# GpSimd's feed-forward sums dealt out one to a slot, and four expert units gathered by transfers instead of products

## The chip, the core and the metric

The kernel runs on one core of a Trainium2 chip. A core has five engines with instruction queues of their own: TensorE (PE; its weight loads are shown as PEld), VectorE (DVE), ScalarE (ACT), GpSimd (POOL) and SyncE (SP). Here SP issues nearly all transfers from memory. The metric is the device time of one launch in microseconds. Everything is computed in fp32.

## What is computed

A two-layer transformer block is followed by a second block whose layers end in a mixture of experts. Two parts of it matter here. The first is the squared-ReLU feed-forward at the end of each of the first block's two layers:

```python
h2 = _rmsnorm(h_res, ln2_g[layer])
h_res = h_res + jnp.square(jax.nn.relu(h2 @ w_ff1[layer])) @ w_ff2[layer]
```

The second is the routed part of the two mixtures of experts: 256 tokens, 64 experts, six experts for each token.

```python
def step(acc, xs):
    e, rt, rw = xs
    xb = xf[rt]                                       # the rows of the tokens that chose expert e
    hb = jax.nn.silu(xb @ w_gate[e]) * (xb @ w_up[e])
    yb = (hb @ w_down[e]).astype(F32) * rw[:, None]
    return acc.at[rt].add(yb), None
```

A token is a row of 1024 numbers, and an expert's gate, up and down weights are 1 MiB each.

## The kernel before

**The feed-forward: 32 slots a layer.** Each of the two products is cut into 16 slots, 32 in all, numbered n. A slot multiplies one 1 MiB piece of weights by seven products in place of eight (Strassen's scheme, in a form that reuses partial sums). So it needs combinations of the four quarters of its weights ("mixed") and of the four quarters of the activations ("sums"). In a slot TensorE makes 28 matmuls, in seven groups of four. They begin once VectorE has joined the results of slot n-2, the third group waits for VectorE's `("mixed", L, n)`, and the last group but one waits for GpSimd's.

Per slot, VectorE adds up the seven results (`joined`, L1929 to L1940, four operations, each of which reads PSUM). Then it makes two of the four weight combinations of slot n+2 (`mixed`, L1912 and L1914), the first of which waits for GpSimd's first one. In three slots of four it also does one part of an unrelated job, the modulation weights of the second block (`ada_part`, two operations of 1024 columns, L1712), with a small bias addition after the third (L1717). GpSimd makes the other two weight combinations of each slot (L3170, L3171) as soon as the weights have landed and slot n-2 has been used. In slots 5, 9, 13 and 17 it also combines eight rows of the activations that slots 0 to 15 have produced, in four operations (L3179, L3181, L3182, L3184). Slots 16 to 19 are the first that read those.

SP issues the weights in groups of four slots (L3244), each once slot n-4 is used. Behind each group it waits for VectorE to have finished the last three `ada_part`s and then issues three more MiB of modulation weights (L3249). Its queue is in order.

**The experts: 27 units a layer.** Unit u (0 to 26) handles 128 gathered rows in groups of 32. Each unit has a kind that says how many experts share its 128 rows: `HALVES` (two experts, 64 rows each), `MOST` (two experts, 96 and 32) or `FOUR` (four experts). Units 1 to 25 are five bodies of five, of the kinds HALVES, FOUR, MOST, MOST, HALVES. A unit on TensorE is: the gate and up products of its own rows; the down product of unit u-1; the gather of the rows for unit u+1, in two halves with an `add_up` between them that adds unit u-2's results into the tokens; the row numbers of unit u+2; the other `add_up`; and the transposition of the hidden values. VectorE copies the row numbers out (L2438) and, for a unit that gathers by transfer, also writes them as indices (L2443), which releases GpSimd's indirect transfer (L3209). That transfer goes into one buffer, `M_XT`, and is at most one unit ahead.

A gather is made in one of two ways. By products: eight matmuls of 128 columns in each half, of the tokens in SBUF with a matrix of ones and zeros (L600). By transfer: the 128 rows are fetched from memory and turned with four transpositions in each half (L605). `one_hot(u)` says which. In unit 3 of each body (u = 8, 13, 18, 23) the gather for the next unit, when made by products, is put ahead of the down product:

```python
ahead = one_hot(u + 1) and u > SHARED_UP and (u - 1) % len(BODY) == AHEAD_OF_DOWN
```

Unit 2 also makes tables, unit 3 the shared expert's up product and unit 4 its down product.

The expert weights come through a ring of 13 slots of 1 MiB. SP issues load n once the load n-13 has been used by TensorE (L3298), in order. A body needs 36 loads.

Of the kernel before, what the change touches and what calls it, by code (L numbers as in the profile page):

```python
# [71 lines left out]

def one_hot(u):

    return 1 < u < UNITS - 1 and (u - 1) % len(BODY) in ONE_HOT_PLACES


def fetches(u):
# [209 lines left out]
def build(nc, io, out_ap, known):  # L288
# [2861 lines left out]
    def gpsimd_program():  # L3150
        PE, VE, AC = PES[0], VES[0], ACS[0]
        for L in range(DEPTH):
            if L:
                po.wait_ge(VE.sem, VE.of("ff2 ends", L - 1))
            po.wait_ge(PE.sem, PE.of("x square sums", L))
            POS.up(po.memset(QTM, 0.0))
            POS.up(po.memset(KTM, 0.0), "mla zeroed", L)
            po.wait_ge(PE.sem, PE.of("mla", L, MLA_H - 1, "out"))
            POS.up(po.memset(DQ, 0.0))
            POS.up(po.memset(DK, 0.0), "diff zeroed", L)  # L3160
            for n in range(32):
                po.wait_ge(*dense.landed(FF_AT[L] + n))
                if n == 0:
                    po.wait_ge(VE.sem, VE.of("o normed", L))
                elif n == 1:
                    po.wait_ge(VE.sem, VE.of("attended", L, 4))
                else:
                    po.wait_ge(PE.sem, PE.of("ff used", L, n - 2))
                b11, b12, b21, b22 = quarters(FF_AT[L] + n)
                POS.up(po.tensor_tensor(MIXED[n % 2][0], b12, b11, ALU.subtract), "mixed 1", L, n)  # L3170
                POS.up(po.tensor_tensor(MIXED[n % 2][2], b22, b12, ALU.subtract), "mixed", L, n)  # L3171
                if n in (5, 9, 13, 17):
                    i = (n - 5) // 4
                    t0, t1, width = halves(L)
                    rows = F[:, 8 * i:8 * i + 8, :]
                    a11, a12, a21, a22 = rows[:, 0:4, t0], rows[:, 4:8, t0], rows[:, 0:4, t1], rows[:, 4:8, t1]
                    s1, s2, s4 = [x[:, i, :, 0:width] for x in (S_ONE, S_TWO, S_FOUR)]
                    po.wait_ge(AC.sem, AC.of("ff1 squared", L, 4 * i + 3))
                    POS.up(po.tensor_tensor(s1, a21, a22, ALU.add))  # L3179
                    po.wait_ge(POS.sem, POS.n)  # L3180
                    POS.up(po.tensor_tensor(a21, a11, a21, ALU.subtract))  # L3181
                    POS.up(po.tensor_tensor(s2, s1, a11, ALU.subtract))  # L3182
                    po.wait_ge(POS.sem, POS.n)
                    POS.up(po.tensor_tensor(s4, a12, s2, ALU.subtract), "ff2 sums", L, i)  # L3184
        po.wait_ge(VE.sem, VE.of("even rb", 2))
        po.wait_ge(AC.sem, AC.of("even rb", 3))
        po.dma_start(skew, E_RB).then_inc(skew_stored, 16)
        po.wait_ge(skew_stored, 16)
        for h in range(4):
            for o, n, c0 in ((255, P, 0), (127, 2 * P, P)):  # L3190
                src = bass.AP(tensor=skew.tensor, offset=512 * h + o, ap=[[4 * 512 - 1, P], [1, n]])
                po.dma_start(E_BIAS[:, h, c0:c0 + n], src).then_inc(skew_loaded, 16)

        def moe_layer(L):
            PE, VE, AC = PES[L], VES[L], ACS[L]
            if L == 0:
                po.wait_ge(VE.sem, VE.of("even mix"))
            else:
                po.wait_ge(PE.sem, PE.of("odd o", 1, 1, 1))
            POS.up(po.memset(M_XT, 0.0), "tokens zeroed", L)  # L3200
            for t in range(2):
                po.wait_ge(AC.sem, AC.of("ht", L, t, 1))
                po.dma_start(tokens[L][t * P:(t + 1) * P], M_HT[:, t, :]).then_inc(tokens_stored[L], 16)
            po.wait_ge(POS.sem, POS.of("tokens zeroed", L))
            po.wait_ge(tokens_stored[L], 32)

            def fetch(column):

                po.indirect_dma_start(M_XT, None, tokens[L],  # L3209
                                      bass.IndirectOffsetOnAxis(M_IX[:, column:column + 1], 0), bounds_check=SEQ - 1,  # L3210
                                      oob_is_err=False).then_inc(tokens_landed[L], 16)

            def numbers_made():
                po.wait_ge(numbered[L], 1)
                po.sem_clear(numbered[L])

            po.wait_ge(first_numbered[L], 1)
            fetch(1)
            with po.Fori(0, fetches(UNITS) - 1) as i:
                numbers_made()  # L3220
                fetch(0)
            po.wait_ge(VE.sem, VE.of("turns", L))
            turns = po.value_load(NTI[0:1, L:L + 1], min_val=1, max_val=1 + NOV // 2)
            with po.Fori(0, turns) as i:
                numbers_made()
                fetch(0)

        for L in range(DEPTH):
            moe_layer(L)
# [181 lines left out]
```

## Time and profile before

| | us |
|---|---|
| median of 3 runs | 2589.15 |
| lowest and highest | 2588.43 and 2592.13 |
| the profiled execution, its own time | 2594.4 |
| its span, from first to last instruction | 2593.1 |

The profiled execution is 5.3 us above the median, and 1.3 us of it lie outside the span. The feed-forward slots lie at about 366 to 582 us of the span (first layer) and 916 to 1130 us (second). The units 1 to 26 of the experts lie at about 1321 to 1794 us and at 2094 to 2566 us.

### The profile page before, as it was taken

What the parts mean: (1) busy time and instruction counts of PE and PEld (TensorE: products, weight loads), DVE (VectorE), ACT (ScalarE), POOL (GpSimd) and SP (SyncE); (2) the same over time, 40 slices, a digit from 0 to 9 for tenths busy, and PEclk for the clock granted to TensorE, in tenths of its full rate; (3) what the DMA queues carried; (4) which work ended last, traced back from release to release, by engine and by line L of the source; (5) the groups of instructions that cost most, each with busy time, mean ns of one, the idle gap of its engine ahead of it and who ended that gap; (6) DMA issues with size and microseconds to landing.
All of it is one profiled execution on the core that took longest, in us unless ns stands there. A gap on an engine that the chain in (4) does not pass through costs nothing.

```text
span 2593.1 us, 50004 instructions
## 1 busy us (share of the span) xinstructions
PE 2523.5 (97%) x21294; PEld 1976.6 (76%) x21294; DVE 1102.9 (43%) x2368; ACT 506.7 (20%) x1110; POOL 277.3 (11%) x213
## 2 busy tenths in 40 slices
PE   9999999999999999999999999999999899999998
PEld 6787789997788899988866666665888766666665
DVE  4546448875455378853321111112674321111112
ACT  2323312102333122011210111111342210111102
POOL 0000016630000046410000000000000000000000
PEclk9999999999999999999899999999999999999999
DMA  5223346763233466755389999996331589999995
GB/s 201 95 98 114 114 180 259 293 255 122 95 112 115 145 269 254 310 201 221 145 335 380 390 420 419 419 420 277 116 114 51 227 349 375 400 420 419 419 420 206
DMA packets 96028, 659.58 MB, mean 254 GB/s; under 512 B 12878, under 2 KB 14430, under 8 KB 17728
## 3 DMA queue, kind: packets, MB, share of 16 engines
q1 hardware_dynamic: 90736, 647.28, 62.8%
q0 software_dynamic: 4784, 8.80, 1.0%
q8 instruction: 169, 2.77, 0.4%
q14 instruction: 51, 0.42, 0.0%
q10 hardware_dynamic: 288, 0.31, 0.0%
HBM read 660.92 MB, written 4.19 MB: 256 GB/s over the span
## 4 chain that ended last, share of the span: by engine, by line
PE 89%; DVE 3%; DMA 3%; POOL 2%; ACT 2%; issue 1%; SPq 0%; DVEq 0%; POOLq 0%; ACTq 0%
PE PS L600 85%; PE PS L605 4%; ACT AR L2613 1%; DMA AR<-in_experts 1%; DMA wmoe<-in_experts 1%; DMA wdense<-in_experts 1%; DVE wmoe L1712 1%; DVE wmoe L1912 1%; POOL AR L3181 1%; DVE wmoe L1914 1%; DMA wdense<-in_dense 0%; POOL AR L3179 0%; POOL wmoe L3170 0%; POOL AR L3182 0%; POOL wmoe L3184 0%
## 5 line engine op out<-in xcount | busy, mean ns | idle before, releaser
L600 PE MATMUL PS<-H,wdense 128*128 128x256 f32 (+4 forms) x2432 | 515.3, 368 | 6.4 <-ACT H L2613 2.2
L600 PE MATMUL PS<-AR 128*128 128x128 f32 (+12 forms) x4848 | 498.7, 312 | 14.9 <-ACT AR L2613 10.0
L600 PEld LDWEIGHTS PS<-H,wdense 128*128 128x128 f32 (+1 forms) x2432 | 422.7, 192 | 75.2 <-issue 10.6
L600 PEld LDWEIGHTS PS<-AR 128*32 128x32 f32 (+5 forms) x4848 | 353.2, 148 | 134.7 <-issue 71.5
L2613 ACT ACTIVATE AR<-PS 128x256 f32<-128x256 f32 (+11 forms) x433 | 185.6, 437 | 1343.5 <-PE PS L600 999.4
L600 PE MATMUL PS<-wmoe,AR 128*32 128x256 f32 (+4 forms) x3280 | 343.7, 413 | 5.8 <-DMA wmoe<-in_experts 5.6
L600 PE MATMUL PS<-AR,wdense 128*128 128x256 f32 (+3 forms) x1472 | 283.6, 348 | 2.2 <-DVE AR L2359 2.2
L600 PE MATMUL PS<-AR,CST 128*128 128x256 f32 (+3 forms) x1096 | 271.6, 387 | 12.8 <-ACT AR L2613 12.8
L600 PEld LDWEIGHTS PS<-AR,wdense 128*128 128x128 f32 x1472 | 243.9, 191 | 33.1 <-DVE AR L2359 3.1
L600 PE MATMUL PS<-wdense,AR 128*32 128x256 f32 (+7 forms) x2112 | 257.0, 420 | 1.8 <-DMA wdense<-in_experts 1.3
L600 PEld LDWEIGHTS PS<-wmoe,AR 128*32 128x32 f32 (+2 forms) x3280 | 166.0, 119 | 116.4 <-issue 51.8
L600 PEld LDWEIGHTS PS<-AR,CST 128*128 128x128 f32 (+1 forms) x1096 | 194.3, 189 | 49.6 <-issue 11.1
L600 PEld LDWEIGHTS PS<-wdense,AR 128*32 128x32 f32 (+3 forms) x2112 | 119.1, 118 | 85.6 <-issue 40.9
L2537 DVE TENSOR_TENSOR AR<-AR,PS 128x256 f32<-128x256 f32 x54 | 22.8, 421 | 365.6 <-ACT AR L2613 365.6
L600 PE MATMUL PS<-wdense,H 128*16 128x64 f32 (+3 forms) x1632 | 168.7, 285 | 0.0
L600 PE MATMUL PS<-AR,wmoe 128*128 128x136 f32 (+5 forms) x1472 | 155.6, 271 | 10.3 <-DVE wmoe L1914 10.1
L600 PEld LDWEIGHTS PS<-wdense,H 128*16 128x16 f32 (+1 forms) x1632 | 141.2, 137 | 21.3 <-issue 4.1
L600 PEld LDWEIGHTS PS<-AR,wmoe 128*128 128x128 f32 (+3 forms) x1472 | 140.1, 174 | 20.0 <-DVE wmoe L1914 11.6
L3170 POOL TENSOR_TENSOR wmoe<-wdense 128x512 f32<-128x512 f32 x64 | 89.5, 1398 | 600.9 <-DMA wdense<-in_dense 420.9
L2613 ACT ACTIVATE AR<-AR 128x272 f32<-128x272 f32 (+13 forms) x207 | 124.1, 621 | 106.1 <-DVE AR L1841 40.1
L1712 DVE SCALAR_TENSOR_TENSOR wmoe<-wmoe 128x1024 f32<-128x1024 f32 x96 | 130.8, 1401 | 0.0
L3209 POOL DMA_INDIRECT AR<-tokens,IX x26 | 25.9, 996 | 970.2 <-DVE IX L2443 940.7
(318 smaller groups left out, 2049.1 us busy)
## 6 DMA issues: line engine op xcount, KB each, us to landing
wmoe<-in_experts SPq DMA_DIRECT2D x180, 1024.0 KB, 17.1
wdense<-in_dense SPq DMA_DIRECT2D x172, 1024.0 KB, 4.8
wdense<-in_experts SPq DMA_DIRECT2D x114, 1024.0 KB, 17.7
AR<-in_experts SPq DMA_DIRECT2D x90, 1024.0 KB, 17.1
wmoe<-in_ada SPq DMA_DIRECT2D x48, 1024.0 KB, 8.4
AR<-in_dense SPq DMA_DIRECT2D x4, 1024.0 KB, 7.5
tokens<-AR POOLq DMA_DIRECT2D x4, 512.0 KB, 4.0
wdense<-in_dense SPq DMA_DIRECT2D x2, 768.0 KB, 9.3
```

Source lines behind the costliest of these rows:

```text
L600: return te.matmul(out, lhsT, rhs, start=start, stop=stop, skip_group_check=True)
L605: return te.matmul(out, src, ident[0:n, 0:n], start=True, stop=True, is_transpose=True, skip_group_check=True)
L1712: VE.up(ve.scalar_tensor_tensor(w, w, 1.0, CROW, ALU.mult, ALU.mult, accum_out=MODS[:, at(2 * s + g, 1)]))
L1912: VE.up(ve.tensor_tensor(m2, b22, m1, ALU.subtract))
L1914: VE.up(ve.tensor_tensor(m4, b21, m2, ALU.subtract), "mixed", L, n)
L2537: VE.up(ve.tensor_tensor(M_HM, M_HM, PS[:, B_GU, 0:256], ALU.mult))
L2613: return ac.activation(dst, src, f, bias=bias, scale=scale)
L3170: POS.up(po.tensor_tensor(MIXED[n % 2][0], b12, b11, ALU.subtract), "mixed 1", L, n)
L3181: POS.up(po.tensor_tensor(a21, a11, a21, ALU.subtract))
L3209: po.indirect_dma_start(M_XT, None, tokens[L], bass.IndirectOffsetOnAxis(M_IX[:, column:column + 1], 0), bounds_check=SEQ - 1, oob_is_err= ...
```

## The change

GpSimd's four operations for a block of eight activation rows no longer stand together in slots 5, 9, 13 and 17. One stands behind the two weight combinations of each slot from 5 on. The last block has two in slot 17 and two in slot 18. The other edit is `one_hot`: units 2, 3, 4 and 24 are now gathered by transfer, so that 11 units of a layer instead of 15 are gathered by products. Unit 23 no longer gathers ahead of its down product.

```diff
-    return 1 < u < UNITS - 1 and (u - 1) % len(BODY) in ONE_HOT_PLACES
+    return len(BODY) < u < UNITS - 3 and (u - 1) % len(BODY) in ONE_HOT_PLACES
```

```diff
-                if n in (5, 9, 13, 17):
-                    i = (n - 5) // 4
+                if 5 <= n < 19:
+                    i, r = (n - 5) // 4, (n - 5) % 4
...
-                    po.wait_ge(AC.sem, AC.of("ff1 squared", L, 4 * i + 3))
-                    POS.up(po.tensor_tensor(s1, a21, a22, ALU.add))
-                    po.wait_ge(POS.sem, POS.n)
-                    POS.up(po.tensor_tensor(a21, a11, a21, ALU.subtract))
-                    POS.up(po.tensor_tensor(s2, s1, a11, ALU.subtract))
-                    po.wait_ge(POS.sem, POS.n)
-                    POS.up(po.tensor_tensor(s4, a12, s2, ALU.subtract), "ff2 sums", L, i)
+                    steps = [(s1, a21, a22, ALU.add), (a21, a11, a21, ALU.subtract), (s2, s1, a11, ALU.subtract), (s4, a12, s2, ALU.subtract)]
+                    if r == 0:
+                        po.wait_ge(AC.sem, AC.of("ff1 squared", L, 4 * i + 3))
+                    for j in (range(2 * r, 2 * r + 2) if i == 3 else range(r, r + 1)):
+                        out, x, y, how = steps[j]
+                        if j in (1, 3):
+                            po.wait_ge(POS.sem, POS.n)
+                        POS.up(po.tensor_tensor(out, x, y, how), "ff2 sums", L, i)
```

GpSimd's queue in the first layer, slots 5 and 6 before (L3170 and L3171 are a slot's weight combinations, the others are the four sums):

```order
L3170 TENSOR_TENSOR wmoe<-wdense 128x512
L3171 TENSOR_TENSOR AR<-wdense 128x512
L3179 TENSOR_TENSOR AR<-AR 128x544
L3181 TENSOR_TENSOR AR<-AR 128x4x136
L3182 TENSOR_TENSOR AR<-AR 128x544
L3184 TENSOR_TENSOR wmoe<-AR 128x544
L3170 TENSOR_TENSOR wmoe<-wdense 128x512
L3171 TENSOR_TENSOR wmoe<-wdense 128x512
```

and slots 5 to 8 after, where the sums are all line L3185:

```order
L3170 TENSOR_TENSOR wmoe<-wdense 128x512
L3171 TENSOR_TENSOR AR<-wdense 128x512
L3185 TENSOR_TENSOR AR<-AR 128x544
L3170 TENSOR_TENSOR wmoe<-wdense 128x512
L3171 TENSOR_TENSOR wmoe<-wdense 128x512
L3185 TENSOR_TENSOR AR<-AR 128x4x136
L3170 TENSOR_TENSOR wmoe<-wdense 128x512
L3171 TENSOR_TENSOR AR<-wdense 128x512
L3185 TENSOR_TENSOR AR<-AR 128x544
L3170 TENSOR_TENSOR wmoe<-wdense 128x512
L3171 TENSOR_TENSOR wmoe<-wdense 128x512
L3185 TENSOR_TENSOR wmoe<-AR 128x544
```

The same four sums now have a pair of weight combinations between each two of them.

TensorE's queue at the end of unit 1, where the rows of unit 2 are gathered (AR x AR is the product with ones and zeros, CST is the unit matrix of a transposition or a result in `add_up`):

```order
-L600 MATMUL PS<-AR 128x128 x8
-L600 MATMUL PS<-AR,CST 128x256 x4
-L600 MATMUL PS<-AR 128x128 x8
+L605 MATMUL PS<-CST,AR 128x128 x4
+L600 MATMUL PS<-AR,CST 128x256 x4
+L605 MATMUL PS<-CST,AR 128x128 x4
 L600 MATMUL PS<-AR 32x2 x8
```

Sixteen matmuls became eight transpositions in the same place. It is the same in units 2 and 3.

In unit 23 the sixteen stood between the gate and up products and the down product (the operations of 512 columns):

```order
 L600 MATMUL PS<-wdense,AR 32x256 x33
-L600 MATMUL PS<-AR 128x128 x16
 L600 MATMUL PS<-wdense,AR 32x512
 L600 MATMUL PS<-wmoe,AR 32x512 x3
```

They left that place, and the eight transpositions stand behind the down product, around `add_up`. VectorE gets one operation more, L2443, in units 0, 1, 2 and 22, and GpSimd one indirect transfer more behind each.

## Rows read from the trace of the kernel before

**Rows 1.** Waits of TensorE: for whom; us in total, times, longest.
```profile
PE PS L600 <- DVE wmoe L1914: 10.1, 8, 1.4
PE PS L600 <- DMA wmoe<-in_experts: 5.6, 2, 2.8
```

**Rows 2.** Timeline of TensorE, feed-forward: start, us, instruction, [idle before <- releaser].
```profile
437.74 1.19 PE L600 MATMUL PS<-AR,wmoe 128*128 128x136 f32 x8 [1.18 <-DVE wmoe L1914]
...
468.94 1.09 PE L600 MATMUL PS<-wmoe,wdense 128*128 128x136 f32 x8
...
475.43 1.09 PE L600 MATMUL PS<-wmoe,wdense 128*128 128x136 f32 x8
```

**Rows 3.** Timeline of GpSimd, slots 9 and 10 of the first layer.
```profile
426.35 1.64 POOL L3179 TENSOR_TENSOR AR<-AR 128x544 f32<-128x544 f32 x1 [1.97 <-ACT AR L2613]
428.06 2.21 POOL L3181 TENSOR_TENSOR AR<-AR 128x544 f32<-128x544 f32 x1
...
431.65 1.34 POOL L3184 TENSOR_TENSOR wmoe<-AR 128x544 f32<-128x544 f32 x1
432.96 1.26 POOL L3170 TENSOR_TENSOR wmoe<-wdense 128x512 f32<-128x512 f32 x1
```

**Rows 4.** Timeline of VectorE in the same slots.
```profile
425.57 1.22 DVE L1712 SCALAR_TENSOR_TENSOR wmoe<-wmoe 128x1024 f32<-128x1024 f32 x1
...
426.71 2.35 DVE L1712 SCALAR_TENSOR_TENSOR wmoe<-wmoe 128x1024 f32<-128x1024 f32 x1
...
430.42 0.44 DVE L1934 TENSOR_TENSOR AR<-AR,PS 128x272 f32<-128x272 f32 x1
...
434.26 1.75 DVE L1912 TENSOR_TENSOR wmoe<-wdense,wmoe 128x512 f32<-128x512 f32 x1 [2.12 <-POOL wmoe L3170]
...
439.45 0.68 DVE L1912 TENSOR_TENSOR AR<-wdense,wmoe 128x512 f32<-128x512 f32 x1
```

**Rows 5.** L3244's weight load issued at 430.4, the first behind three modulation loads.
```profile
DMA to landing us min/median/max: 12.2/12.2/12.2
```

**Rows 6.** Timeline of VectorE, experts: copies of row numbers, one per unit (0, 5 to 9).
```profile
1320.70 0.16 DVE L2438 COPY AR<-PS 128x2 f32<-128x2 f32 x1 [1.41 <-PE PS L600]
...
1420.99 0.16 DVE L2438 COPY AR<-PS 128x2 f32<-128x2 f32 x1 [2.30 <-PE PS L600]
...
1439.36 0.16 DVE L2438 COPY AR<-PS 128x2 f32<-128x2 f32 x1 [5.06 <-PE PS L600]
...
1457.86 0.16 DVE L2438 COPY AR<-PS 128x2 f32<-128x2 f32 x1 [5.06 <-PE PS L600]
...
1477.58 0.15 DVE L2438 COPY AR<-PS 128x2 f32<-128x2 f32 x1
...
1493.19 0.15 DVE L2438 COPY AR<-PS 128x2 f32<-128x2 f32 x1
```

**Rows 7.** Timeline of TensorE: the first half of a gather, by products and by transpositions.
```profile
1331.42 2.05 PE L600 MATMUL PS<-AR 128*128 128x128 f32 x16
...
1489.98 0.66 PE L605 MATMUL PS<-CST,AR 128*128 128x128 f32 x4
```

**Rows 8.** Windows, first layer's experts: stretch, busy us by engine, clock, DMA share, GB/s.
```profile
1320.00:1405.00 85.00, 85.00 (x870) 58.65 (x868) 15.96 (x49) 7.80 (x17) 1.01 (x1) 1.00 1.00 413
1405.00:1452.00 47.00, 47.00 (x455) 29.41 (x449) 9.02 (x24) 5.25 (x11) 0.99 (x1) 1.00 0.84 323
1452.00:1712.00 260.00, 254.87 (x2688) 165.81 (x2686) 47.10 (x123) 29.04 (x59) 5.93 (x6) 1.00 1.01 420
```

**Rows 9.** GpSimd's 26 indirect transfers, line L3209.
```profile
DMA to landing us min/median/max: 2.1/8.1/9.3
```

**Rows 10.** Expert load issued at 1733.7 (second down weights of unit 23).
```profile
DMA to landing us min/median/max: 21.1/21.1/21.1
```

**Rows 11.** Timeline of TensorE: a down product, and unit 24's gather behind its down product.
```profile
1391.60 3.62 PE L600 MATMUL PS<-AR 128*32 128x512 f32 x32
...
1759.88 0.66 PE L605 MATMUL PS<-CST,AR 128*128 128x128 f32 x4
```

## The prediction

> **What bounds the kernel now.** I read the waits of TensorE first, then the timelines of the two places that the change touches, then how fast the transfers run there. TensorE is busy nearly all the time, so time can only be won where TensorE waits, or by taking work from it. Of the waits two bear on this change [rows 1]: 10.1 us in eight waits for VectorE's second weight combination (L1914), and 5.6 us in two waits for expert weights. The eight waits are one for each of the four bunches of sums in each of two layers. At 426.35 GpSimd starts its four sums for slot 9, at 432.96 it is at last at the weights of slot 10 [rows 3], VectorE begins its part of them at 434.26 [rows 4], and TensorE stands for 1.18 us until 437.74 [rows 2]. A slot without a wait is 6.5 us (468.94 to 475.43, the same group of matmuls one slot apart [rows 2]), so four slots are 26.0 and a period with one bunch of sums 27.3.
>
> The expert stage has two bounds that lie close together. By TensorE a unit of the second body takes 15.6 to 19.7 us [rows 6]. The transfers run at 413 GB/s from 1320 to 1405, at 323 from 1405 to 1452, and at 420 from there on, which is all they ever give [rows 8]. So at first TensorE sets the pace and later the transfers do.
>
> **Part one, gathers: TensorE's side.** Unit 6 gathers by products and takes 18.37 us (1420.99 to 1439.36), unit 9 by transfer and takes 15.61 (1477.58 to 1493.19) [rows 6]: 2.76 us less. The halves say the same: 2.05 us busy against 0.66 [rows 7], twice 1.4. Three units of the first body (1, 2 and 3, which gather for 2, 3 and 4) make 3 x 2.75 = 8.2 us in a layer. Unit 23 has today's form of unit 8, with the products ahead of the down product: 19.72 us (1457.86 to 1477.58) [rows 6]. It becomes like unit 9, 4.1 us less. Together 12.3 us less work for TensorE in a layer.
>
> **Part one: what the transfers let through.** The 36 loads of a body do not get fewer, so TensorE's 8.2 us count only if the transfers still have time to spare before they saturate. From 1320 to 1405 they leave (420 - 413)/420 x 85 = 1.4 us unused, from 1405 to 1452 (420 - 323)/420 x 47 = 10.9 [rows 8], together 12.3. The change takes 8.2 of that away. It adds three token transfers of 0.5 MB, at 420 GB/s 1.25 us each if they cost their bytes, 3.7 in all. 8.2 + 3.7 = 11.9 is less than 12.3: the gain passes in full, and everything behind it, the saturated stretch too, starts 8.2 us earlier. It is a close sum, though. Had the spare time been 8 us, nearly half of the gain would be gone. A bound from the other end is a token transfer that costs nothing, with 4.1 us to spare and the same 8.2.
>
> For unit 23 the transfers are saturated. The second down weights of unit 23 were issued at 1733.7 and landed 21.1 us later [rows 10], at 1754.8. TensorE asks for them when unit 24's down product starts, at 1759.88 less 3.6 = 1756.3 [rows 11]. So they are 1.5 us early, and of the 4.1 us only 1.5 come through; the rest turns into a wait for a transfer. Ends: 0 and 4.1.
>
> Do the fetched rows come in time? Unit 1 is the tightest, since it has one `add_up` less in front. Its row numbers are copied at 1320.70 [rows 6] and its gather starts at 1331.42 [rows 7], 10.7 us later. A fetch takes 8.1 us from issue to landing, 9.3 at most [rows 9], which leaves 1.4 to 2.6 us for VectorE's index write and GpSimd's start. I cost the wait at 0; at the other end it is 1 us in a layer. The write and the start lie on engines that are nearly idle here (16.0 and 1.0 us busy of 85 [rows 8]), and TensorE has 12 us of other work meanwhile. Should the wait come, the slots of the ring behind it come free later by as much.
>
> On that transfer the Trainium skill gives a formula (DMA: Bandwidth & Descriptors, "Anatomy of one DMA"): about 2.0 us plus the bytes over 436 GB/s, for half a MiB an estimate of 3.2 us. The trace disagrees, with its 8.1 us among expert loads, and only its 2.1 us at the least would fit an idle queue. By the page the rows could never be late; by the trace they just aren't, and the measurement decides.
>
> Gathers in all: -(8.2 + 1.5) = -9.7 us a layer, -19.4 for both.
>
> **Part two, the sums dealt out.** At first sight this wins all 10.1 us: a slot has 6.5 us, GpSimd's two weight combinations take 2.5 of them (1.26 each) and one sum 1.34 more [rows 3]. But GpSimd and VectorE stop each other. VectorE's modulation step takes 1.22 us alone; the one that starts at 426.71 takes 2.35 [rows 4]. It ends at 429.06, and GpSimd's L3179 ended at 427.99 [rows 3]: it did nothing until then and took its 1.07 us after. In turn L3181 takes 2.21 us, where L3184 takes 1.34: it began at 428.06 and got going when VectorE ended. L1912 takes 1.75 us beside GpSimd and 0.68 alone, while the `joined` operations keep their 0.44 beside it (430.42) [rows 4]: they read PSUM. So operations of the two engines that only read SBUF run one after the other, and each meeting costs VectorE up to 1.1 us.
>
> VectorE's work in four slots, alone: four `joined` of 4 operations (up to 0.44, with gaps 1.7) 6.8; four pairs of combinations (0.68 each) 5.6; six modulation steps of 1.22, 7.3; gaps and the bias step 0.9. That is 20.6 us of 26.0. I laid out the queues of both engines slot by slot in either order, with these durations and that rule. In the old order VectorE waits 5.4 us for GpSimd in a period; 20.6 + 5.4 = 26.0 fits into 27.3, and the layout gives the TensorE wait as 1.30 us a bunch, against 1.18 in the row [rows 2]. In the new order every sum stands where VectorE is in its second combination or in a modulation step, and the waits are 6.8, 7.4 and 8.7 us in the first three periods. 20.6 + 7.4 = 28.0 does not fit into 26.0. VectorE falls back by 2 us a period. For two periods nobody sees it, and TensorE wins 1.3 us twice. In the third TensorE must wait for `joined` (results of slot n-2) and the period is 28.8. In the fourth, with its two sums in slots 17 and 18, it is 27.7 against 27.2. In slot 21 TensorE then waits 2.0 us. First layer: -1.3 - 1.3 + 1.5 + 0.5 + 2.0 = +1.4. In the second layer, where a slot is 0.23 us shorter and VectorE's work hardly less, the same layout gives +3.2. Sum +4.6, which I round to +5.
>
> The sums themselves come early enough: the last two stand behind the weights of slot 18, and slot 19 is the first that reads them. GpSimd's wait for ScalarE (1.97 us [rows 3]) stays in slots 5, 9, 13 and 17, with one sum behind it in place of four.
>
> What gets late next is known too. SP issues three modulation loads only after VectorE's last step of the four, and the next weights stand behind them: 12.2 us from issue to landing [rows 5], against the two slots, 13.0 us, until GpSimd can use them. Every us by which VectorE falls back passes nearly whole into those weights. A landing 1.2 us late makes the sum 3 us worse in a layer. Bounds of part two: -10.1 (no meeting matters) and +11 (VectorE falls back and the weights come late in both layers). I take +5, since it is by these very rows; it lies between.
>
> The Trainium skill has this as a rule (SBUF — State Buffer, "Who interferes with whom"): GpSimd and a VectorE operation with two SBUF inputs share a port pair as an exclusive lock, held for the whole instruction, and the other one blocks. The trace agrees, with 2.35 for 1.22 us.
>
> **Sum.** The profiled execution took 2594.4 us, span 2593.1: 2594.4 - 19.4 + 5.0 = 2580.0. It lies 5.3 above the median of the runs, so against that median 2589.15 - 14.4 = **2574.7**.
>
> **Rivals.**
> 1. *The sums leave the path for good*: the meetings happen but VectorE catches up where it has no modulation step. For it: one slot in four has none. Against it: the balance of 28.0 us against 26.0. 2589.15 - 19.4 - 10.1 = 2559.6.
> 2. *Late weights*: VectorE's delay comes back through SP's queue, part two costs +11. For it: 12.2 of 13 us [rows 5]. 2580.7.
> 3. *Part two is nought, or unit 23's 4.1 us come through*: 2570.
> 4. *The other side: the transfers bind from the start of the units.* Then TensorE's 12.3 us only lengthen its waits for loads, and eight fetches of 1.25 us are added to a stream that is full: +10, with part two +15, 2604. It decides at the spare transfer time: 12.3 us now, 11.9 needed; it would need fewer than 4. Against it: 323 GB/s from 1405 to 1452 [rows 8].
>
> **How the numbers follow.** The forecast 0.50, rival 1 0.20, rival 2 0.15, rival 3 0.09, rival 4 0.06. The forecast's own range, with the ends of unit 23 and of the fetches, is 2568 to 2580. To leave no more than 2 in 10 out, the range goes from rival 1 to a little above rival 2: 2559 to 2583. About 0.2% (5.2 us) is what a measurement can tell from no change. Faster by more: 0.88; within: 0.06; slower: 0.06.
>
> **What would show it.** Right: 64 more transpositions (L605) and 128 fewer products of 128 columns (L600); units 1, 2 and 3 are 2.75 us shorter; the rate from 1405 to 1452 rises towards 420 GB/s; a wait for expert weights of 1 to 3 us appears behind unit 23; L1712 has more operations of 2.3 us than now; TensorE's waits on L1914 do not vanish but move to the later slots, some of them on L1940. Wrong: no waits of TensorE on VectorE in the slots (rival 1), GpSimd waiting for `wdense` in slots 8, 12 and 16 (rival 2), or unit 1 waiting for its tokens.

## The result, and the profile after

The changed kernel takes 2573.85 us (median of 4 runs, 2572.99 to 2576.02), where before takes 2588.79 (4 runs, 2588.37 to 2592.13): 14.9 us less, a ratio of 0.9941 with a 95% interval of 0.9929 to 0.9954. The forecast was 2574.7, 14.4 less than the 2589.15 that it started from.

The two profiled executions differ by more, 2593.1 against 2571.8 of span. So the parts are read stage by stage. First the expert units. Timeline of VectorE, the copies of row numbers at the end of units 0 to 3, 22 and 23, first layer of after (start, us, operation):

```profile
1320.09 0.15 DVE L2438 COPY AR<-PS 128x2 f32<-128x2 f32 x1
1333.94 0.15 DVE L2438 COPY AR<-PS 128x2 f32<-128x2 f32 x1
1350.99 0.15 DVE L2438 COPY AR<-PS 128x2 f32<-128x2 f32 x1
1373.84 0.15 DVE L2438 COPY AR<-PS 128x2 f32<-128x2 f32 x1
...
1718.44 0.15 DVE L2438 COPY AR<-PS 128x2 f32<-128x2 f32 x1
1736.83 0.15 DVE L2438 COPY AR<-PS 128x2 f32<-128x2 f32 x1
```

Units 1, 2 and 3 take 13.85, 17.05 and 22.85 us. Before they took 16.59, 19.79 and 25.59: each is 2.74 shorter, in both layers. Unit 23 takes 18.39 where it took 19.64, and 17.75 in the second layer. (Where VectorE writes the numbers as indices first, L2443, the copy comes 0.08 us later. That is taken out here.) Unit 17 takes 0.67 less in the first layer and 0.89 more in the second, units 22 and 24 up to 0.2 more. The 26 units give 9.96 us in the first layer and 8.94 in the second, 18.9 together.

Only part of this repeats. Nine more traces, of the experiments below, have the same gathers. Units 1 to 3 are as short in every one. Units 17 and 22 to 24 come out otherwise each time, and against the 946.0 us of before the 26 units of both layers give from 14.0 to 18.1 us in them. The 18.9 of after are the most of the ten, and 16.9 is their mean.

Three windows of after, which answer to [rows 8] (stretch, busy us by engine, clock, DMA share, GB/s):

```profile
1320.00:1405.00 85.00, 85.00 (x850) 55.76 (x852) 17.38 (x57) 8.23 (x17) 4.96 (x5) 1.00 1.02 420
1405.00:1452.00 47.00, 47.00 (x456) 30.88 (x454) 9.64 (x24) 5.88 (x12) 0.00 (x0) 1.00 1.00 413
1452.00:1712.00 260.00, 254.12 (x2688) 162.03 (x2676) 46.94 (x121) 27.85 (x57) 5.93 (x6) 0.99 1.01 420
```

The spare time is used up: 413 became 420 and 323 became 413. Of 12.3 us some 0.8 are left. The 34 indirect transfers (line L3210 of after, [rows 9]) now take

```profile
DMA to landing us min/median/max: 2.1/8.6/10.3
```

Now the feed-forward. TensorE's waits in the whole of after, those that answer to [rows 1] (us in total, times, longest):

```profile
PE PS L600 <- DMA wmoe<-in_experts: 10.0, 4, 2.8
PE PS L600 <- DVE wmoe L1914: 8.1, 7, 2.6
...
PE PS L600 <- DVE AR L1940: 4.2, 5, 1.1
PE PS L600 <- DVE AR L1914: 2.7, 4, 1.9
```

On VectorE TensorE waits 15.0 us in the slots, where before it waited 12.0 (10.1, and 1.9 once on L1914 writing `AR`). The waits moved to later slots, and five are now on `joined` (L1940). The timeline of TensorE shows all those of the first layer; the one in slot 6 is gone:

```profile
436.83 1.19 PE L600 MATMUL PS<-AR,wmoe 128*128 128x136 f32 x8 [0.89 <-DVE wmoe L1914]
...
455.85 2.12 PE L600 MATMUL PS<-H,wdense 128*128 128x136 f32 x16 [1.14 <-DVE AR L1940]
...
463.59 2.12 PE L600 MATMUL PS<-H,wdense 128*128 128x136 f32 x16 [0.99 <-DVE AR L1940]
...
466.59 1.19 PE L600 MATMUL PS<-AR,wmoe 128*128 128x136 f32 x8 [0.89 <-DVE wmoe L1914]
...
486.67 2.12 PE L600 MATMUL PS<-AR 128*128 128x136 f32 x16 [0.35 <-DVE AR L1914]
...
496.03 5.51 PE L600 MATMUL PS<-AR,wmoe 128*128 128x136 f32 x32 [2.60 <-DVE wmoe L1914]
...
517.46 2.12 PE L600 MATMUL PS<-AR 128*128 128x136 f32 x16 [0.17 <-DVE AR L1914]
```

GpSimd's waits, first of before and then of after, slots of the first layer:

```profile
POOL wmoe L3170 <- PE PS L600: 92.1, 21, 18.5
POOL AR L3179 <- ACT AR L2613: 6.7, 4, 2.0
POOL wmoe L3170 <- DMA wdense<-in_dense: 5.2, 1, 5.2
```

```profile
POOL wmoe L3170 <- PE PS L600: 71.6, 18, 19.1
POOL wmoe L3170 <- DMA wdense<-in_dense: 16.3, 4, 5.5
POOL AR L3185 <- ACT AR L2613: 13.5, 4, 4.6
```

It now waits for weights in slots 8, 12, 16 and 20, the first of each group of four, which is what the second rival told. How late they are shows beside `early_one_each`, an experiment in which only the order of the loads differs. Slot 8 in `early_one_each`, then in after:

```profile
414.74 1.74 POOL L3170 TENSOR_TENSOR wmoe<-wdense 128x512 f32<-128x512 f32 x1 [2.23 <-PE PS L600]
```

```profile
416.02 1.28 POOL L3170 TENSOR_TENSOR wmoe<-wdense 128x512 f32<-128x512 f32 x1 [3.61 <-DMA wdense<-in_dense]
```

So the weights of slot 8 come 1.3 us late; those of slot 12 come 4.0 late (444.71 against 440.68). What comes of the second wait stands in the timelines of GpSimd and then VectorE around slot 12:

```profile
444.71 1.27 POOL L3170 TENSOR_TENSOR wmoe<-wdense 128x512 f32<-128x512 f32 x1 [5.51 <-DMA wdense<-in_dense]
445.94 1.27 POOL L3171 TENSOR_TENSOR wmoe<-wdense 128x512 f32<-128x512 f32 x1
447.30 1.67 POOL L3185 TENSOR_TENSOR wmoe<-AR 128x544 f32<-128x544 f32 x1
448.93 1.72 POOL L3170 TENSOR_TENSOR wmoe<-wdense 128x512 f32<-128x512 f32 x1
450.60 2.25 POOL L3171 TENSOR_TENSOR AR<-wdense 128x512 f32<-128x512 f32 x1
```

```profile
449.44 2.29 DVE L1712 SCALAR_TENSOR_TENSOR wmoe<-wmoe 128x1024 f32<-128x1024 f32 x1
...
451.66 2.28 DVE L1712 SCALAR_TENSOR_TENSOR wmoe<-wmoe 128x1024 f32<-128x1024 f32 x1
...
454.08 0.44 DVE L1934 TENSOR_TENSOR AR<-AR,PS 128x272 f32<-128x272 f32 x1
```

The combinations of slots 12 and 13 and a sum stand in a row of 8.1 us, and both of VectorE's modulation steps take 2.3 us for 1.22. `joined` begins at 454.08, and that is the wait at 455.85.

How long the slots last is read from VectorE's L1912, from slot 2 to slot 31. Timelines, before and then after, both layers:

```profile
376.61 1.48 DVE L1912 TENSOR_TENSOR wmoe<-wdense,wmoe 128x512 f32<-128x512 f32 x1
...
570.05 1.74 DVE L1912 TENSOR_TENSOR AR<-wdense,wmoe 128x512 f32<-128x512 f32 x1 [1.73 <-POOL wmoe L3170]
...
927.01 1.53 DVE L1912 TENSOR_TENSOR wmoe<-wdense,wmoe 128x512 f32<-128x512 f32 x1
...
1118.53 1.74 DVE L1912 TENSOR_TENSOR AR<-wdense,wmoe 128x512 f32<-128x512 f32 x1 [1.50 <-POOL wmoe L3170]
```

```profile
377.30 1.48 DVE L1912 TENSOR_TENSOR wmoe<-wdense,wmoe 128x512 f32<-128x512 f32 x1
...
575.71 1.74 DVE L1912 TENSOR_TENSOR AR<-wdense,wmoe 128x512 f32<-128x512 f32 x1 [1.73 <-POOL wmoe L3170]
...
934.33 1.53 DVE L1912 TENSOR_TENSOR wmoe<-wdense,wmoe 128x512 f32<-128x512 f32 x1
...
1125.89 1.74 DVE L1912 TENSOR_TENSOR AR<-wdense,wmoe 128x512 f32<-128x512 f32 x1 [1.50 <-POOL wmoe L3170]
```

193.4 became 198.4, and 191.5 became 191.6: the sums dealt out cost 5.0 us. So the traces give -18.9 + 5.0 = -13.9, beside 14.9 less by the medians. The other 7.4 us between the two traces are not the change. Most of them lie at one place between feed-forward and experts, one window of before and then the same of after:

```profile
1280.00:1300.00 20.00, 17.80 (x82) 16.03 (x80) 10.83 (x61) 8.94 (x17) 1.08 (x2) 0.66 0.28 105
```

```profile
1280.00:1300.00 20.00, 16.48 (x105) 13.82 (x104) 14.60 (x73) 11.73 (x26) 1.08 (x2) 1.00 0.25 96
```

The granted clock was 0.66 in before, which by an estimate is 0.34 x 20 = 6.8 us lost, and 1.00 in after.

The other signs: the trace has 64 more L605 (806 for 742) and 256 fewer L600 of 128 columns. It shows each of the 128 products left out as two, as the x16 for eight in [rows 7]. Of VectorE's 96 modulation steps 24 take over 2 us, where 16 did.

### The profile page after: what moved, and what is told of

It is laid out like the page before. It is cut to its first block, busy times and chain, and to the rows that moved or that the text cites. A ratio compares the mean times of both kernels' runs of the same rounds, so it can differ in the third digit from the quotient of the medians.

```text
span 2571.8 us, 49672 instructions
## 1 busy us (share of the span) xinstructions
PE 2497.0 (97%) x21102; PEld 1948.7 (76%) x21102; DVE 1125.0 (44%) x2376; ACT 506.7 (20%) x1110; POOL 301.9 (12%) x221
## 3 DMA queue, kind: packets, MB, share of 16 engines
q8 instruction: 167, 2.74, 0.4%
## 4 chain that ended last, share of the span: by engine, by line
PE 85%; DMA 7%; DVE 5%; ACT 1%; issue 1%; POOL 0%; SPq 0%; DVEq 0%; ACTq 0%
PE PS L600 81%; PE PS L605 4%; DMA wmoe<-in_experts 3%; DMA wdense<-in_dense 3%; DVE wmoe L1712 2%; DMA wdense<-in_experts 1%; ACT AR L2613 1%; DVE wmoe L1912 1%; DVE wmoe L1914 0%; POOL wmoe L3170 0%; DVE AR L1912 0%; DVE AR L1914 0%; ACT ST L2613 0%; SPq L3250 0%; DMA wmoe<-in_ada 0%
## 5 line engine op out<-in xcount | busy, mean ns | idle before, releaser
L600 PE MATMUL PS<-H,wdense 128*128 128x256 f32 (+4 forms) x2432 | 512.0, 366 | 10.6 <-DVE AR L1940 4.2
L600 PEld LDWEIGHTS PS<-H,wdense 128*128 128x128 f32 (+1 forms) x2432 | 420.0, 190 | 79.9 <-issue 10.5
L600 PE MATMUL PS<-AR 128*128 128x128 f32 (+14 forms) x4592 | 466.1, 313 | 13.1 <-ACT AR L2613 8.6
L600 PEld LDWEIGHTS PS<-AR 128*32 128x32 f32 (+5 forms) x4592 | 321.2, 145 | 127.3 <-issue 69.2
L600 PE MATMUL PS<-wmoe,AR 128*32 128x256 f32 (+4 forms) x3280 | 345.3, 415 | 5.5 <-DMA wmoe<-in_experts 5.5
L600 PE MATMUL PS<-AR,wdense 128*128 128x256 f32 (+3 forms) x1472 | 283.6, 348 | 2.2 <-DVE AR L2359 2.2
L600 PE MATMUL PS<-AR,CST 128*128 128x256 f32 (+3 forms) x1096 | 272.2, 388 | 12.7 <-ACT AR L2613 12.7
L600 PEld LDWEIGHTS PS<-AR,wdense 128*128 128x128 f32 x1472 | 243.8, 191 | 33.1 <-DVE AR L2359 3.1
L600 PE MATMUL PS<-wdense,AR 128*32 128x256 f32 (+7 forms) x2112 | 256.9, 420 | 6.9 <-DMA wmoe<-in_experts 4.5
L600 PEld LDWEIGHTS PS<-wmoe,AR 128*32 128x32 f32 (+2 forms) x3280 | 167.0, 120 | 116.8 <-issue 52.8
L600 PEld LDWEIGHTS PS<-AR,CST 128*128 128x128 f32 (+1 forms) x1096 | 194.8, 189 | 48.1 <-issue 11.0
L600 PEld LDWEIGHTS PS<-wdense,AR 128*32 128x32 f32 (+3 forms) x2112 | 119.0, 118 | 91.0 <-issue 46.0
L600 PE MATMUL PS<-wdense,H 128*16 128x64 f32 (+3 forms) x1632 | 169.1, 286 | 0.0
L3170 POOL TENSOR_TENSOR wmoe<-wdense 128x512 f32<-128x512 f32 x64 | 99.7, 1558 | 578.1 <-DMA wdense<-in_dense 436.2
L600 PE MATMUL PS<-AR,wmoe 128*128 128x136 f32 (+5 forms) x1472 | 156.9, 272 | 8.4 <-DVE wmoe L1914 8.1
L600 PEld LDWEIGHTS PS<-wdense,H 128*16 128x16 f32 (+1 forms) x1632 | 141.6, 138 | 21.3 <-issue 4.1
L600 PEld LDWEIGHTS PS<-AR,wmoe 128*128 128x128 f32 (+3 forms) x1472 | 141.4, 175 | 17.9 <-DVE wmoe L1914 9.5
L3210 POOL DMA_INDIRECT AR<-tokens,IX x34 | 33.8, 994 | 943.1 <-DVE IX L2443 913.6
L1712 DVE SCALAR_TENSOR_TENSOR wmoe<-wmoe 128x1024 f32<-128x1024 f32 x96 | 139.7, 1494 | 0.5 <-DMA wmoe<-in_ada 0.4
## 6 DMA issues: line engine op xcount, KB each, us to landing
wmoe<-in_experts SPq DMA_DIRECT2D x180, 1024.0 KB, 18.4
wdense<-in_experts SPq DMA_DIRECT2D x114, 1024.0 KB, 18.5
```

The lines of the kernel that those rows point to most:

```text
L600: return te.matmul(out, lhsT, rhs, start=start, stop=stop, skip_group_check=True)
L1712: VE.up(ve.scalar_tensor_tensor(w, w, 1.0, CROW, ALU.mult, ALU.mult, accum_out=MODS[:, at(2 * s + g, 1)]))
L3210: po.indirect_dma_start(M_XT, None, tokens[L], bass.IndirectOffsetOnAxis(M_IX[:, column:column + 1], 0), bounds_check=SEQ - 1, oob_is_err= ...
```

## The experiments

In the expectations TensorE's waits are counted from start to start of its matmuls (13.4 us in before, 17.9 in after). The view of waits counts them 0.15 to 0.2 us shorter each (12 and 15), and sums of its rounded lines stand in the text and the table below, good to 0.1 or 0.2 us. One kernel's runs differ by up to 20 us, along with their mean granted clock (last section), so the times carry wide intervals, and the stages of the traces decide. Ratios are against before on the same chip.

**Each part alone.** `gathers_alone` is before with the edit of `one_hot` only, `sums_alone` before with the other edit only.

> The kernel before with the edit of one_hot alone: units 2, 3, 4 and 24 gather by transfer, the sums stay in one bunch. Theory: the two parts are independent and add up. The trace of after shows units 1 to 3 each 2.74 us shorter and unit 23 1.25 and 1.89 shorter, 18.9 us for both layers: 2588.8 - 18.9 = 2569.9 us. Rival A (the sums bring the gain, the gathers only shift waits): 2584 us. Rival B (the extra transfers cost what TensorE saves): 2588.

> The kernel before with the sums dealt out alone, all gathers as before. Theory: VectorE and GpSimd stop each other more often and the weights behind the modulation loads come late, so the edit costs 5 us: 2588.8 + 5.0 = 2593.8 us, with TensorE's waits in the slots at 17.9 us in both layers where before has 13.4. Rival (a bunch was what TensorE waited for, so dealing it out must win): 2588.8 - 10.1 = 2578.7 us.

Measured: gathers alone 0.9929 (0.9911 to 0.9947), 18.4 us less. The sums alone 1.0019 (1.0005 to 1.0034), 4.9 us more; the slots of the two layers took 198.7 and 193.1 us, 5.3 and 1.6 longer than in before. The interval of the second ratio goes from 1 to 9 us, so the sign is clear and the size is not. Together they make 13.5 us less, beside the 14.9 of after: within the noise the parts add up. The rivals fall, and the sums lose where they were to win.

**The weights early.** SP loads one slot of weights more ahead of the first modulation loads, so that the first of each later group of four no longer stands behind them:

```diff
             for i in range(4):
-                load(4)
+                load(5 if i == 0 else 4)
                 if i == 0:
                     sp.wait_ge(VE.sem, VE.of("h2", L))
...
             for i in range(4):
-                load(4)
+                load(3 if i == 3 else 4)
                 if i == 0:
                     sp.wait_ge(VE.sem, VE.of("ff1 ends", L))
```

> The changed kernel, but SP issues the weights of the first slot of each group of four (slots 8, 12, 16, ... of the feed-forward) ahead of the three modulation loads and not behind them. Nothing else moves, VectorE and GpSimd have the same operations in the same order. Theory: it is the late weights that cost. In the trace of after GpSimd waits for them before slots 8, 12, 16 and 20 (3.6, 5.5, 5.3, 1.9 us in the first layer), its combinations of two slots and a sum then come in a row and fall on VectorE's modulation steps. With the weights there in time TensorE's waits fall from 17.9 us to about 8 (2.3 and 5.5): 2573.9 - 10 = 2564 us. Rival (what my prediction said: VectorE has 28.0 us of work and waits in 26.0, whenever the weights come): the waits stay, 2572 to 2574 us.

Measured: 0.9901 (0.9882 to 0.9920), 25.6 us below before. TensorE's waits on VectorE fell from 15 to 8.4 us. GpSimd's wait for weights is gone in the first layer. In the second 2.9 us stayed, and VectorE waited for its first modulation load, since load 5 holds it back until slot 0 is used: the edit had a fault of its own. Later modulation loads are late too, as they now stand behind a load of weights: in the second layer VectorE waits for them four times, 8.1 us in all. It had not waited for them in before.

**Small modulation steps.** L1712 over 64 columns in place of 1024.

```diff
-                w = WM[:, s, D * g:D * g + D]
-                VE.up(ve.scalar_tensor_tensor(w, w, 1.0, CROW, ALU.mult, ALU.mult, accum_out=MODS[:, at(2 * s + g, 1)]))
+                w = WM[:, s, D * g:D * g + 64]
+                VE.up(ve.scalar_tensor_tensor(w, w, 1.0, CROW[:, 0:64], ALU.mult, ALU.mult, accum_out=MODS[:, at(2 * s + g, 1)]))
```

> The changed kernel with VectorE's modulation steps over 64 columns in place of 1024, so most of the modulation products is left out of the computation; the transfers and waits stay. Theory (both forms of it): without this work on the shared port nobody meets anybody and all waits of TensorE in the slots go: 2573.9 - 17.9 = 2556 us. Rival (GpSimd's chain alone, two combinations and a sum in a slot, holds TensorE): the waits stay on VectorE's L1914, over 2568 us.

Measured: 0.9872 (0.9851 to 0.9893), and no wait of TensorE on VectorE in any slot; the slots took 187.8 and 181.1 us. GpSimd has the same operations, so TensorE pays for VectorE's modulation steps and what they meet, not for GpSimd's chain. The run does not tell the steps' own time (six times 1.22 us in four slots) from the meetings.

**More and fewer gathers by transfer.** `fetch_bodies` fetches for units 7 to 9 and 12 to 14 too (`3 * len(BODY) < u` in `one_hot`), `keep_unit24` takes unit 24 back to products (`u < UNITS - 1`).

> The changed kernel, and the second and third body gather by transfer too (units 7 to 9 and 12 to 14): TensorE has 2.75 us less to do in each of six more units of a layer, and units 8 and 13 lose the early gather as well. Theory: from 1405 us on the transfers have no time to spare, TensorE's gain turns whole into waits for expert weights, and each fetch adds between 0.6 us (replay) and 1.25 us (0.5 MB at 420 GB/s) to the stream: 6 fetches in two layers, 7 to 15 us slower than after, 2581 to 2589 us. Rival (TensorE still sets the pace): 6 x 2.75 x 2 = 33 us faster, 2541 us.

> The changed kernel with unit 24 gathered by products again, so only the first body is changed. Theory: 4.1 us more work of TensorE in unit 23 of each layer, of which the transfers hid all but 1.25 and 1.89 us: 3.1 us slower, 2577 us, and the waits for the down weights of unit 23 go. Rival (the 4.1 us count in full): 8.2 us slower, 2582 us. Rival (the transfers hide it all): the same, 2573.9 us.

Measured: `fetch_bodies` 0.9980 (0.9967 to 0.9993), some 10 us slower than after by the ratios; the 26 units took 468.4 and 469.3 us, where after has 463.7 and 463.4, 10.6 more; of the ten traces with the gathers of after the longest, 932.0 in both layers, is still 5.7 short of `fetch_bodies`. Its waits for expert weights in the first layer, and below them those of after:

```profile
PE PS L600 <- DMA wdense<-in_experts: 10.8, 2, 7.0
PE PS L600 <- DMA AR<-in_experts: 8.8, 4, 4.1
PE PS L600 <- DMA wmoe<-in_experts: 3.6, 2, 2.5
```

```profile
PE PS L600 <- DMA wmoe<-in_experts: 5.4, 2, 2.8
```

Units 6 and 7 did become 15.6 and 15.8 us long (18.4 and 18.5 in after), and unit 12 became 27.0. The work went from TensorE and came back as waits, with the price of the fetches on top. `keep_unit24`: 0.9953 (0.9937 to 0.9970), 3.1 us slower than after by the ratios, but the intervals overlap. By the units it is 4.8 us slower than after (931.9 for 927.1 in both layers), yet two of the ten traces with the gathers of after have 932.0. Whether the edit of unit 24 wins anything is open.

**How the sums are dealt out, with late and early weights.** `gathers_early` and `early_bunch` keep the bunch. `late_3_1` and `early_3_1` deal three and one. `two_early` is three and one as well, but leaves out the last of a layer's sixteen sums. In `early_bunch`, `early_one_each` and `early_3_1` the fifth load stands in the second group (`5 if i == 1`), so the first modulation loads are not held back.

```diff
-                    for j in (range(2 * r, 2 * r + 2) if i == 3 else range(r, r + 1)):
+                    k = ((0, 2, 4) if i == 3 else (0, 3, 4, 4, 4))
+                    for j in range(k[r], k[r + 1]):
```

> The edit of one_hot and the early weights (first slot of each group ahead of the modulation loads), with the sums in one bunch as before. Theory: the early weights help only where the sums are dealt out, since with a bunch TensorE waits for GpSimd's own 5.4 us of sums (13.4 us in both layers), which no load shortens: as the gathers alone, 2568 to 2570 us, TensorE's waits in the slots still at 11 us or more. Rival (the early weights are worth their 10 us by themselves, and dealing out the sums is worth nothing): 2560 us.

> As after with the early weights, but the sums dealt out otherwise: three behind the combinations of slots 5, 9 and 13 and one behind those of the next, the last block two, one and one. So they end before VectorE's modulation steps of the next slots. From a replay of the queues with the traces' durations: TensorE's waits in the slots 0.9 and 4.0 us in the two layers, against 2.8 and 7.2 measured for one sum a slot with early weights; by the traces more like 1.4 and 5.7. It should be the fastest: 2 to 4 us below the changed kernel with early weights, 22 to 26 below before: 2562 to 2566 where before is 2588. Rival (how they are dealt doesn't matter once the weights are early): the same waits, 10 us.

> The changed kernel with the sums dealt out three and one (three behind the combinations of slots 5, 9, 13, one behind those of the next; the last block two and two), weights loaded in the old order. Theory: the place of the sums decides how often GpSimd falls on the modulation steps, and so how late they end: TensorE's waits in the slots 0.7 to 3.3 us in the first layer and 4.5 to 7.0 in the second (replay, without and with gaps in the stream of transfers), against 8.4 and 9.4 in after; 8 to 12 us below after. Rival (without early weights every way of dealing out is late): 8 and 9 us again.

> The same with the weights of slots 8, 12, 16, ... ahead of the modulation loads, from the second group on, so that the first modulation loads are issued as early as before. Theory: both cures add up, waits of 0 to 1 us in the first layer and under 4 in the second (4.5 with the first group moved too, where VectorE waited 2.0 us for its first modulation load). It should be the fastest of all: 25 us below before, 10 below after.

> The changed kernel (one sum a slot) with the weights ahead of the modulation loads from the second group on. Theory: the waits of the second layer fall from the 7.2 us that they were with the first group moved too to 4 or 5, the first layer stays at 2.8; 10 us below after. Rival (it was the late weights alone, and the place of the sums is nothing): as early as three and one.

> The edit of one_hot alone with the weights ahead of the modulation loads from the second group on, the sums in one bunch. Theory: with a bunch TensorE waits for GpSimd's 5.4 us, which no load shortens: 5.2 us of waits in the first layer as before, 6.8 to 8.2 in the second, the same time as with the gathers alone. The 3.5 us wait that came up in the second layer, when the first group was moved too, is gone.

TensorE's waits on VectorE in the slots, first and second layer, and the length of the slots from 2 to 31, in us. Falls are those of TensorE's granted clock in the slots, each of which costs some 1.7 us of the length (the last section has them):

| kernel | sums | weights | waits | slots | falls | ratio (95%) |
|---|---|---|---|---|---|---|
| before | bunch | late | 4.5, 7.4 | 193.4, 191.5 | 0, 1 | 1 |
| gathers_alone | bunch | late | 4.5, 7.8 | 193.5, 190.3 | 0, 0 | 0.9929 (0.9911 to 0.9947) |
| gathers_early | bunch | early, first group too | 4.5, 7.8 | 193.5, 193.9 | 0, 1 | 0.9942 (0.9922 to 0.9962) |
| early_bunch | bunch | early | 4.5, 5.5 | 193.6, 189.6 | 0, 0 | 0.9928 (0.9911 to 0.9944) |
| after | one each | late | 7.0, 8.1 | 198.4, 191.6 | 1, 0 | 0.9941 (0.9929 to 0.9954) |
| after_early | one each | early, first group too | 2.2, 6.2 | 191.1, 192.6 | 0, 1 | 0.9901 (0.9882 to 0.9920) |
| early_one_each | one each | early | 2.2, 5.1 | 191.1, 190.6 | 0, 1 | 0.9897 (0.9878 to 0.9916) |
| late_3_1 | three, one | late | 4.3, 5.6 | 195.4, 192.0 | 1, 2 | 0.9923 (0.9902 to 0.9944) |
| early_3_1 | three, one | early | 0.3, 3.1 | 189.4, 189.0 | 0, 1 | 0.9908 (0.9885 to 0.9931) |

`two_early` had 0.9884 (0.9867 to 0.9902), waits of 0 and 3.6 us, and 188.5 and 189.7 us of slots; with one sum fewer it is only a bound for `early_3_1`. Two forecasts missed: `late_3_1` was to be 8 to 12 us below after and is 5 below, with overlapping intervals and more waits in the first layer (4.3) than the 0.7 to 3.3 expected, and the waits of `early_bunch` in the second layer fell to 5.5 where 6.8 to 8.2 were expected.

GpSimd's waits in the first layer of `early_one_each`, beside those of after above: no wait for weights, and the combinations stand apart again.

```profile
POOL wmoe L3170 <- PE PS L600: 82.0, 25, 18.5
POOL AR L3185 <- ACT AR L2613: 7.9, 4, 2.4
```

What follows. Early weights do nothing in the first layer for a bunch, take 4.8 of 7.0 us from one sum a slot, and 4.0 of 4.3 from three and one. The place alone takes 2.7 there (7.0 to 4.3). In the second layer even the bunch gains 1.9: before had one wait of that size there (at 1060.7), 13 us behind a wait of 6.5 us of GpSimd for weights, and with early weights both are gone. In `gathers_early` VectorE stood for its first modulation load of the second layer:

```profile
DVE wmoe L1712 <- DMA wmoe<-in_ada: 2.1, 1, 2.1
```

and a wait of 3.4 us of TensorE came of it, which `early_bunch` has not. Early weights have a price as well: in the second layer of `early_one_each` VectorE waits 1.5 us for a modulation load at 1038.1, and TensorE's longest wait of that trace, 2.5 us at 1045.6, comes behind it. By waits and slots `early_3_1` is the best kernel, 3.4 us of waits for 15 in after; its slots are 11.6 us shorter. By time `early_3_1` and `early_one_each` can't be told apart, at 24 and 27 us below before. The interval of `early_one_each` lies clear below that of after, 4 to 5 thousandths lower in the middle; that of `early_3_1` overlaps it by a little.

## Why the prediction was right, and where it was right by luck

**Units 1 to 3.** 2.75 us each was forecast, 2.74 measured, six times. The spare time of 12.3 against 11.9 us held, and of it 0.8 us are left. `fetch_bodies` shows that it was a real limit: six units further the same edit costs time.

**Unit 23: right by luck.** 1.5 us of 4.1 was forecast, 1.25 and 1.89 measured in after. But in `gathers_alone`, with the same gathers, it was 1.98 in the first layer and nothing in the second, and in seven of the ten traces unit 23 of the first layer is longer than the 19.64 us of before (19.8 to 21.95). By the mean of the ten it gives nothing in the first layer and 1.5 us in the second. Where the transfers set the pace, the length of one unit tells little. Units 4 to 26 give 0.4 us by the mean, in both layers together, where I had 3.0. In after the wait that takes the rest stands one product earlier than I wrote: in unit 23 itself, 2.57 us at 1730.05 for the down weights of unit 22.

```profile
1730.05 0.59 PE L600 MATMUL PS<-wdense,AR 128*32 128x512 f32 x1 [2.57 <-DMA wmoe<-in_experts]
```

**The fetched rows in time.** Costed at 0. The longest fetch now takes 10.3 us, longer than the 9.3 that I reckoned with, and units 1 to 3 are as short as forecast; one weight load (L605) waited 0.8 us for its tokens, in the second layer. On a transfer the measurement stays far from the formula of the Trainium skill (DMA: Bandwidth & Descriptors, "Anatomy of one DMA"), which gives an estimate of 3.2 us: 8.6 in the median.

**The sums, +5.** The size was right: 5.0 by the slots, 4.9 by `sums_alone` (6.9 by its slots). That is luck in part, since the cause below is another. The split was not right: +1.4 and +3.2 was forecast, +5.0 and 0.0 measured. 1.7 us of each error are the clock: it fell behind the wait of 2.6 us at 496 in after, and behind a wait of 1.9 us at 1061 in the second layer of before. Without it the layers stand at +3.2 and +1.8. The first waits of TensorE came a period sooner than in my layout (0.9 us in slot 10, where I had none) and the largest in slot 18 (2.6) in place of slot 21.

**The cause was only half right.** The step that failed is the one that lets the new order cost VectorE more than the old, 6.8 to 8.7 us a period for 5.4, and with it "20.6 + 7.4 = 28.0 does not fit into 26.0". The timelines of the first layer, from slot 4 to slot 20 (four periods), give what VectorE spends there on its modulation steps, its weight combinations and its waits for GpSimd, in us:

| kernel | 26 steps | 32 combinations | waits for GpSimd | together |
|---|---|---|---|---|
| before, a bunch | 38.5 | 35.4 | 9.1 | 83.0 |
| `early_one_each` | 42.4 | 38.9 | 1.4 | 82.7 |
| after | 44.7 | 40.0 | 4.1 | 88.8 |

Undisturbed they would be 26 x 1.22 + 16 x (0.68 + 0.69) = 53.6. So GpSimd costs VectorE 29.4 us with a bunch (7.3 a period, where my layout had 5.4) and 29.1 with one sum a slot and the weights on time: the meetings take what the waits give. TensorE then waits 7.3 us in both layers, less than the 10.0 of a bunch, and against `early_bunch` the slots are 2.4 us shorter in the first layer, where I had +1.4, and 1.0 longer in the second with one fall of the clock more, where I had +3.2. With late weights it is 35.2, and there TensorE waits.

How it comes to that can be followed in the traces. SP issues the first modulation loads that wait for VectorE's steps 25.1 us after slot 2 in before and in after alike (401.73 and 402.42): at first VectorE's third step is not pushed back at all. But TensorE no longer waits 1.2 us in slot 6, so the buffers come free earlier, and the weights of slot 8, in before just in time (issued at 403.05, used at 415.39, with 12.0 us on the way), are 1.3 us late. GpSimd bunches up behind them, its operations fall on VectorE's steps, and the next modulation loads, with the weights queued behind them, come later by more each time: 28.4, 29.8 and 30.7 us apart in after, where before has 27.4, 27.4 and 29.8 and `early_one_each` 28.0, 25.9 and 27.8. This circle costs the 7.8 us of waits between `early_one_each` and after. I had kept it apart as a rival with 6 us more. It happened, at the price that I had set for the forecast. It needs the modulation steps all the same: with small ones every wait is gone.

That a VectorE operation with two inputs in SBUF and a GpSimd operation that reads SBUF contend, as the Trainium skill says (SBUF — State Buffer, "Who interferes with whom"), shows in after too: 2.29 and 2.28 us for 1.22. The number of such meetings does not tell the loss: `early_one_each` has 29 steps of over 2 us in both layers, after 24, and its TensorE waits half as long.

**Open.** How TensorE's 7.8 us divide between late weights as such and the meetings that they bring, since neither was changed without the other. Of the 6.1 us that VectorE loses more in the table, 2.7 are waits for GpSimd and 3.4 longer operations. In the second layer it loses only 1.1 more, where TensorE waits 3.0 more. No run took away the meetings and left VectorE its work.

## What to carry to other kernels

A transfer queued behind one that waits for an engine inherits every delay of that engine. Before a wait is taken away, look at what was only just in time because of it, and put the more urgent transfer ahead; then look at what it delays in turn. Work taken from the compute engine counts only as far as the transfers have spare time, which can be read off beforehand: one less rate over full rate, times the stretch. Where the transfers set the pace, read a gain from several traces and not from one unit of one. A sum of waits hides their sizes, so look for the longest too: in these traces those of about 2 us and more often had a fall of the clock behind them.

## What the runs showed of the hardware that I had not expected

**A wait of 2 us costs 1.7 us more, often.** The window of after behind its wait of 2.6 us, the four us ahead of it and those behind (columns as above, the clock third from the end):

```profile
492.00:496.00 4.00, 1.43 (x13) 1.22 (x11) 3.27 (x2) 0.00 (x0) 3.92 (x4) 0.97 0.90 332
496.00:500.00 4.00, 3.97 (x21) 3.97 (x22) 3.99 (x3) 0.00 (x0) 4.00 (x3) 0.60 1.01 426
500.00:504.00 4.00, 4.00 (x37) 4.00 (x36) 3.97 (x7) 0.00 (x0) 2.07 (x2) 1.00 1.01 426
```

TensorE ran at its lower level (1.2 GHz) for 3.4 us and then at 2.4 again. That is an estimate of 1.7 us lost. Over the slots of all fourteen traces two starts of TensorE stood 2.0 us or more apart at 19 places, with waits of 1.83 to 3.39 us. At 13 of them the granted clock fell like this. It fell nowhere else in the slots, so not behind the shorter waits, of which the longest was 1.65 us. So a wait of 2.6 us with its fall (4.3) is dearer than four of 0.9 (3.6), which the sum of waits does not tell. Even the longest does not always bring it: none of the three in `fetch_bodies`, one of them of 2.59 us, did.

**The clock goes with the spread of the runs.** Between feed-forward and experts, where TensorE waits up to 2.2 us at a time, the fall lasted 13.6 us in before (by an estimate 6.8 us lost), as in four of the other traces, and did not come at all in after. From slot 31 of the second layer to the row numbers in unit 0 of the experts after took 193.8 us and before 201.8. The runs of `early_3_1` went from 2556.96 us at a mean clock of 0.995 to 2575.58 at 0.988: 0.007 of 2566 us are 18 us, of the 18.6 between them.
